# Prompt attention in 64 equal steps: query tiles m and 15-m of a head side by side, with the halves of q and k made in the projections

## What is computed

```python
def stick_breaking(q, k, v, sb_bias, q_pos, k_pos):
    z = jnp.einsum('bqhd,bkhd->bhqk', q.astype(jnp.float32), k.astype(jnp.float32)) * (HEAD_DIM_SB ** -0.5)
    z = z + sb_bias.astype(jnp.float32)[None, :, None, None]
    mask = k_pos[None, :] < q_pos[:, None]
    log_1mb = jnp.where(mask, jax.nn.log_sigmoid(-z), 0.0)
    suffix = lax.cumsum(log_1mb, axis=3, reverse=True) - log_1mb
    a = jnp.where(mask, jnp.exp(jax.nn.log_sigmoid(z) + suffix), 0.0)
    o = jnp.einsum('bhqk,bkhd->bqhd', a, v.astype(jnp.float32))
    return o.astype(v.dtype)
```

## Time and profile before

| | us |
|---|---|
| median of three runs | 3154.99 |
| the profiled execution | 3153.76 |
| its span | 3152.2 |
| attention, first logits to first matmul of the next stage | 547.78 to 1198.92 |
| PE busy over the span | 3035.5 (96%) |
| DVE, ACT busy over the span | 2062.2, 1645.0 |

### The profile page before, as it was taken

The page is one execution under the profiler, slowest core; times in us unless marked ns, Lnnn a source line. Parts: engine busy times, 40 slices in busy tenths (PEclk is TensorE's granted clock), DMA queues, the critical chain, the costliest instruction groups (busy, mean ns, idle before and its releaser), DMA issues.

```text
span 3152.2 us, 51506 instructions
## 1 busy us (share of the span) xinstructions
PE 3035.5 (96%) x18364; PEld 2805.3 (89%) x18364; DVE 2062.2 (65%) x2820; ACT 1645.0 (52%) x2375; POOL 149.1 (5%) x277
## 2 busy tenths in 40 slices
PE   8999999888888889999999999999999999999998
PEld 6888887776677669999999999999999999999998
DVE  4222422888987897775677756777477774778845
ACT  5444311997888885543445534455344543444433
POOL 0000000112311220000000000000000000000000
PEclk9999999999999999999999999999999999999999
DMA  5224334554755555443364334543445434444432
GB/s 185 93 93 137 108 114 120 139 135 133 202 129 134 137 169 156 118 120 112 110 183 120 114 114 130 164 119 111 116 142 154 115 113 117 143 127 120 115 112 78
DMA packets 584224, 405.90 MB, mean 129 GB/s; under 512 B 38489, under 2 KB 547842, under 8 KB 584034
## 3 DMA queue, kind: packets, MB, share of 16 engines
q1 hardware_dynamic: 543012, 301.45, 33.8%
q0 software_dynamic: 20544, 67.19, 7.4%
q10 hardware_dynamic: 20512, 35.17, 3.2%
HBM read 358.87 MB, written 44.87 MB: 128 GB/s over the span
## 4 chain that ended last, share of the span: by engine, by line
PE 62%; DVE 0%; issue 0%; DVEq 0%; ACT 0%; ACTq 0%
PE pf_acc L60 20%; PE pf_acc L58 20%; PE pf_acc L59 20%; PE pf_ps_t L1720 1%; PE pf_ps_sum L1659 0%; PE pf_ps_sum L1668 0%; PE pf_ps_sum L1673 0%; PE pf_ps_t L1730 0%; PE pf_ps_t L1791 0%; DVE late_c L2066 0%; DVE late_ssum L1998 0%; DVEq L1596 0%; DVE late_u L1988 0%; DVE pf_h L2192 0%; ACT late_sq L1819 0%
## 5 line engine op out<-in xcount | busy, mean ns | idle before, releaser
L1812 ACT ACTIVATE late_w_hi<-ahead_raw 128x1024 fp32r<-128x1024 f32 x439 | 463.8, 1057 | 536.7 <-PE pf_acc L60 533.9
L60 PE MATMUL pf_acc<-pf_x_hi,late_w_lo 128*128 128x416 f32 x2080 | 734.1, 353 | 0.0
L58 PE MATMUL pf_acc<-pf_x_hi,late_w_hi 128*128 128x416 f32 x2080 | 733.1, 352 | 0.0
L59 PE MATMUL pf_acc<-pf_x_lo,late_w_hi 128*128 128x416 f32 x2080 | 726.0, 349 | 0.0
L1982 DVE TENSOR_TENSOR late_w_lo<-ahead_raw,late_w_hi 128x1024 fp32r<-128x1024 f32 x439 | 536.1, 1221 | 269.8 <-ACT late_w_hi L1812 269.0
L58 PE MATMUL pf_acc<-late_f_hi,late_w_hi 128*128 128x416 f32 x1280 | 453.4, 354 | 3.2 <-DVEq L2205 3.2
L60 PE MATMUL pf_acc<-late_f_hi,late_w_lo 128*128 128x416 f32 x1280 | 451.9, 353 | 0.0
L59 PE MATMUL pf_acc<-late_f_lo,late_w_hi 128*128 128x416 f32 x1280 | 447.6, 350 | 0.0
L59 PEld LDWEIGHTS pf_acc<-pf_x_lo,late_w_hi 128*128 128x128 f32 x2080 | 390.8, 188 | 7.9 <-issue 1.6
L58 PEld LDWEIGHTS pf_acc<-pf_x_hi,late_w_hi 128*128 128x128 f32 x2080 | 390.5, 188 | 3.7 <-issue 1.6
L60 PEld LDWEIGHTS pf_acc<-pf_x_hi,late_w_lo 128*128 128x128 f32 x2080 | 390.0, 187 | 2.3
(11 more groups left out here) (248 smaller groups left out, 3971.9 us busy)
## 6 DMA issues: line engine op xcount, KB each, us to landing
ahead_raw<-in_w_up_dram SPq DMA_DIRECT2D x220, 512.0 KB, 4.0
ahead_raw<-in_w_down_dram SPq DMA_DIRECT2D x80, 512.0 KB, 4.0
high_pages<-in_cache_k_dram POOLq DMA_DIRECT2D x128, 256.0 KB, 3.5
ahead_raw<-in_w_out_dram SPq DMA_DIRECT2D x40, 512.0 KB, 5.3
ahead_raw<-in_w_ple_gate_dram SPq DMA_DIRECT2D x40, 512.0 KB, 4.0
high_pages<-in_cache_v_dram POOLq DMA_DIRECT2D x64, 256.0 KB, 3.4
at_kT<-in_cache_v_dram POOLq DMA_DIRECT2D x64, 256.0 KB, 4.1
ahead_raw<-in_w_down_dram SPq DMA_DIRECT2D x40, 384.0 KB, 3.5
```

The lines of the kernel that those rows point to most:

```text
L58: nc.tensor.matmul(out, stat_hi, mov_hi, start=first, stop=False)
L59: nc.tensor.matmul(out, stat_hi, mov_lo, start=False, stop=False)
L60: return nc.tensor.matmul(out, stat_lo, mov_hi, start=False, stop=last)
L1812: nc.scalar.activation(w_hi[k % 4][:, :], raw[k % 4][:, :], ACT.Copy).then_inc(hi_split, 1)
```

## The change

- A step has two query tiles of a head, m and 15-m, side by side in one row of 17 key blocks: the long tile's keys first, then the short one's. There are 64 steps of 2176 columns, in three pieces of 1024, 1024 and 128 (GRANULES). In heads 0 to 6 the pairs go from (7, 8) to (0, 15), in the last head the other way round.
- A logits chunk in which the border between the tiles lies is made in two parts. Each step has two running products and one multiplication. A result is copied out and stored after every two steps.
- The halves of q and k are made in the projection: `turned` casts and subtracts out of PSUM, four tensors QH, QL, KH, KL are stored, and `load_operands` loads them ready for use, 1536 keys of head 0 in the projection stage, the rest of it at the start of the attention, other heads whole. The raw buffers and all operand work in the attention are gone; so are the bias columns of each head.
- The sample units are spread evenly over steps 3 to 61. With two units in most iterations, eight sums fall into iterations 26 and 55 each.
- Turns and logits take turns (one group, one piece) instead of both pieces in a row, and the weighing of a pair comes right behind them.
- The work on the first tokens' mixture moves from iterations STEPS to STEPS+2 to iterations STEPS+LAG and behind, and its load waits for the stores of pairs 28 and 29.

```diff
 
+FIRST_KEYS = 1536
+
+
+def load_operands(eng, D, tiles, h, cols, loaded):
+
+    q2, k_hi, k_lo = (f32(t[:, cols]) for t in tiles)
+    rows = slice(64 * h, 64 * h + 64)
+    for part in range(2):
+        half = slice(64 * part, 64 * part + 64)
+        eng.dma_start(q2[half, :], D[("QH", "QL")[part]][rows, cols]).then_inc(loaded, 16)
+        eng.dma_start(k_hi[half, :], D["KH"][rows, cols]).then_inc(loaded, 16)
+        eng.dma_start(k_lo[half, :], D["KL"][rows, cols]).then_inc(loaded, 16)
+
+
...
-                sp.dma_start(dst[:, :, bass.ds(at, P)], src[s][:, :, :]).then_inc(stored[s], 16)
+                sp.dma_start(to_hi[:, :, bass.ds(at, P)], hi[s][:, :, :]).then_inc(stored[s], 16)
+                sp.dma_start(to_lo[:, :, bass.ds(at, P)], lo[s][:, :, :]).then_inc(stored[s], 16)
...
             def turned(n, s, which, stores):
-                signal, ready, src, dst, stored, own = (
-                    (k_turned, kT_ready, ps_kT, kT, kT_stored, keep["kT_s"]) if which == "k" else
-                    (q_turned, qT_ready, ps_qT, qT, qT_stored, keep["qT_s"]))
+                signal, high, ready, src, hi, lo, stored, own = (
+                    (k_turned, kT_high, kT_ready, ps_kT, kT, kT_lo, kT_stored, keep["kT_s"]) if which == "k" else
+                    (q_turned, qT_high, qT_ready, ps_qT, qT, qT_lo, qT_stored, keep["qT_s"]))
                 dve.wait_ge(signal, n + 1)
                 if isinstance(n, int) and n == 0:
                     nc.vector.tensor_copy(own[:, :, :], src[:, :].rearrange("p (k t) -> p k t", k=4)[:, :, 0:32]).then_inc(ready, 1)
                     return
                 if stores is not None:
-                    dve.wait_ge(stored[s], 16 * stores)
-                nc.vector.tensor_copy(dst[s][:, :, :].rearrange("p k t -> p (k t)"), src[:, :]).then_inc(ready, 1)
+                    dve.wait_ge(stored[s], 32 * stores)
+                banked = src[:, :].rearrange("p (k t) -> p k t", k=4)
+                nc.vector.tensor_copy(hi[s][:, :, :].bitcast(F32R), banked).then_inc(high, 1)
+                dve.wait_ge(high, n)
+                nc.vector.tensor_tensor(lo[s][:, :, :].bitcast(F32R), banked, hi[s][:, :, :], ALU.subtract).then_inc(ready, 1)
 
             prepare(0, 0, None, 16)
 
@@ -853,14 +869,7 @@
...
     HEADS, NQ, LAG = 8, 16, 3
-    STEPS = HEADS * NQ
+    PER = NQ // 2
+    STEPS = HEADS * PER
+    TILES, GRANULES, RUNS = NQ + 1, 3, 5
...
+    def short_tile(s):
+
+        return s % PER if s // PER == HEADS - 1 else PER - 1 - s % PER
+
+    def long_tile(s):
+        return NQ - 1 - short_tile(s)
...
-    total_keys = sum(keys_of(s) + 300 for s in range(3, STEPS - 2))
     units_of = [[] for _ in range(STEPS + LAG + 2)]
-    t, run, placed = 3, keys_of(3) + 300, 0
+    t, placed, first_unit, last_unit = 3, 0, 3, STEPS - 3
     for g in range(GROUPS):
         for u in range(UNITS):
             if apart(u) and units_of[t]:
-                for _ in range(2 if u in (U_TURN, U_MIX) else 1):
-                    t += 1
-                    run += keys_of(t) + 300
-            while t < STEPS - 3 and run * GROUPS * UNITS < placed * total_keys:
+                t += 2 if u in (U_TURN, U_MIX) else 1
+            while t < last_unit and (t + 1 - first_unit) * GROUPS * UNITS < placed * (last_unit - first_unit):
                 t += 1
-                run += keys_of(t) + 300
...
+    def turns(t):
 
         s = t - LAG
-        return min(groups[s], max(1, 3 - len(turned_fills(t)))) if has(s) else 0
+        if not has(s):
+            return [range(0)] * (GRANULES + 1)
+        first = max(1, 3 - len(turned_fills(t)))
+        ends = [first, first + 1, first + 2, RUNS]
+        return [range(a, b) for a, b in zip([0] + ends, ends)]
 
...
+                def load(h):
+                    if h >= 2:
+                        sp.wait_ge(z_ready, granule(PER * (h - 1), 0))
+                    load_operands(sp, D, [t[h % 2] for t in (q2, k_hi, k_lo)], h, slice(0, 2048), qk_loaded[h % 2])
 
                 def load_v(h):
                     sp.dma_start(v[h % 2][:, :, :].unsqueeze(2), v_src[:, :, h:h + 1, :]).then_inc(v_loaded[h % 2], 16)
...
+                def load_raw():
+                    sp.wait_ge(z_ready, granule(STEPS - PER, 0))
                     for n in range(4):
                         sp.dma_start(join["raw"][n][:, :].rearrange("p (k n) -> p k n", k=8),
                                      T["w_out"][0].rearrange("(k p) n -> p k n", p=P)[:, :, n * P:(n + 1) * P]).then_inc(join["raw_loaded"][n], 16)
-                    sp.wait_ge(half_ready, 2 * HEADS)
-                    sp.wait_ge(oT_stored[0], 32 * 2 * HEADS)
+
+                def load_mix():
+
+                    for n in range(2):
+                        sp.wait_ge(oT_stored[n], 32 + 32 * 15)
                     sp.dma_start(join["mix"][:, :, :], D["MIXT"].rearrange("(k p) t -> p k t", p=P)[:, :, 0:416]).then_inc(join["mix_loaded"], 16)
 
...
                     if h + 1 < HEADS:
-                        load(2 * h + 2)
+                        load(h + 1)
+                    else:
+                        load_raw()
...
-                        load(2 * h + 3)
-                    else:
-                        load_ahead()
-                    store(h, 2)
                     if h + 1 == HEADS:
                         wait_emptied(sp, ("mix", GROUPS - 1))
                         sp.dma_start(D["MIXT"][0:512, 2048:2080].rearrange("(k p) t -> p k t", p=P), mixT[:, :, :]).then_inc(mix_stored, 16)
+                        load_mix()
+                    store(h, 2)
...
                 def logits(s, g):
-                    i, h = s % NQ, s // NQ
-                    n = keys_of(s)
-                    if i == 0 and g == 0:
-                        pe.wait_ge(half_ready, 2 * h + 1)
-                    if i == 8 and g == 0:
-                        pe.wait_ge(half_ready, 2 * h + 2)
+                    h = s // PER
+                    if g == 0 and s % PER == 0:
+                        pe.wait_ge(qk_loaded[h % 2], 96 * (h // 2 + 1) + (96 if h and h % 2 == 0 else 0))
+                    if g == 0 and s == FIRST_KEYS // P - PER:
+                        pe.wait_ge(qk_loaded[0], 192)
                     at = granule(s, g)
                     z = ps_z[at % 2]
                     pe.wait_ge(b_done, at + 1)
-                    width = min(n - 1024 * g, 1024)
-                    for c in range(0, width, BANK):
-                        w = max(min(BANK, width - c), 2 * P)
-                        k0 = 1024 * g + c
-                        diagonal = k0 <= n - P < k0 + w
-                        q = q2[h % 2][:, i * P:(i + 1) * P]
-                        nc.tensor.matmul(z[:, c:c + w], q, k_hi[h % 2][:, k0:k0 + w], start=True, stop=False)
-                        last = nc.tensor.matmul(z[:, c:c + w], q, k_lo[h % 2][:, k0:k0 + w], start=False, stop=not diagonal)
-                        if diagonal:
-                            d = n - P - 1024 * g
-                            last = nc.tensor.matmul(z[:, d:d + P], ident_b[:, :], far_b[:, :], start=False, stop=True)
+                    border = P * (long_tile(s) + 1)
+                    for c in range(1024 * g, min(1024 * (g + 1), WIDTH), BANK):
+                        end = min(c + BANK, WIDTH)
+                        parts = [(c, min(end, border), long_tile(s), c)] if c < border else []
+                        if border < end:
+                            parts.append((max(c, border), end, short_tile(s), max(c, border) - border))
+                        parts.sort(key=lambda part: part[1] - part[0])
+                        for a, b, tile, k0 in parts:
+                            w, z0 = max(b - a, 2 * P), a - 1024 * g
+                            turned = b - a == P and b - c == BANK
+                            last = scores(z, z0 - P if turned else z0, w, q2[h % 2][:, tile * P:(tile + 1) * P], h, k0, turned, b in (border, WIDTH))
+                            if b in (border, WIDTH):
+                                last = nc.tensor.matmul(z[:, b - P - 1024 * g:b - 1024 * g], ident_b[:, :], far_b[:, :], start=False, stop=True)
                     last.then_inc(z_ready, 1)
 
                 def turn(s, r):
                     bank = claim(("turn", s, r))
-                    for kt in range(4 * r, min(4 * r + 4, s % NQ + 1)):
-                        last = nc.tensor.transpose(bank[:, kt % 4 * P:kt % 4 * P + P], rest[s % 4][:, kt * P:(kt + 1) * P], keep["ident"][:, :])
+                    for n in run_tiles(r):
+                        last = nc.tensor.transpose(bank[:, n % 4 * P:n % 4 * P + P], rest[s % 4][:, n * P:(n + 1) * P], keep["ident"][:, :])
                     last.then_inc(filled, 1)
 
...
-                    i, h, quad = s % NQ, s // NQ, s // 4
-                    if i == 0:
+                    h, pair = s // PER, s // 2
+                    if s % PER == 0:
```

(54 more changed lines are left out.)

211 lines of the change are left out of this document (74 added, 137 removed).

## The result

The changed kernel takes 3225.8 us (median of 4 runs, 3223.8 to 3227.8), the kernel before 3155.1: a ratio of 1.022 [1.021, 1.024], slower by 70.7 us. The forecast was 3145 us, and its range ended at 3180. The profiled run has a span of 3225.9 us (before 3152.2).

The account below looks back on a forecast made before the run. No single engine bounds the attention; the most loaded one changes twice in every head. Terms: -17.7 to the last logits, +5.4 attention end, +2 projection end, sum -10.3: 3145 us. Own range 3125 to 3160; with the large rivals 3105 to 3180.

Parts of the forecast that it names:

- One with eight sums on a heap (14): Attention, step into which the planner puts eight sums of the sample part: claimed to take 14 us.
- a heap that meets a weighing, 17: End of the attention, second heap of sums, in a step with a weighing: with two empty steps, put at 17 us.
- Heads' loads grow from 2 to 3 MB; they start four steps ahead, nothing.: Attention, operand loads on SP: start 40 us ahead, cost nothing; sharing engines with the pages 0 to 5 us, taken as 0.
- key step: Attention, 33 steps holding sample key units (1.94 a step): taken as 10.2 us each, ends 9.5 and 10.6, 337 us together.
- The layout: Two key steps laid out, with 0.2 us a hand-over and a weighing every second step: 21.2 us, 10.6 each.
- The step with the new rows: Attention, step for the sample part's new rows, occurring twice: 8 us each.
- that with the sample's scan: Attention, step with the sample scan, occurring twice: 11 us each, DVE 7.2 + 1.2 + 4.4, partly absorbed by its lead.
- End of the projection: Behind the projection's last matmul, two more operations of 0.7 us and one more issue: +2 us (1 to 3).
- End of the attention: Last logits to first token-stage matmul: mixture work moves behind ACT's last copies, 31.3 us against 25.9, +5.4 us (0 to 8).
- TensorE's additional 8 to 22 us: Attention, 46 pairs of logits matmuls a head instead of 40, more of them short: PE's need grows by 8 to 22 us.
- The lump decides: Rival, key steps: 10.6 us holds and PE's waits cost clock, 0.4 us more in 61 steps; 3180 us, chance 0.22.
- The levels even out: Rival, attention: every step runs like the old long half, ACT busy 94%, stage 568 us; 3105 us, chance 0.22.

Follow-up runs that it names:

- e2: Changed kernel without loading 96 of its 128 value pages; sums from the fifth of a group on reread the first four's pages; 3171.2 us, one run.
- e5: e1 with heads' operands from the third on loaded in three parts and the attention's first load on GpSimd's queue; 3169.8 us, ratio 1.004.
- e8: e1 with most of the weighing left out, only the first and last block of each tile multiplied (wrong result); 3140.5 us, one run.
- e9: e5 with two groups of weights turned, not one, ahead of the second logits in steps with sample key units; 3135.2 us, ratio 0.994.
- e6: Changed kernel (64 steps of pairs) without the sample part of the attention; 493.6 us first to last logits, 3030.8 us in all, one run.
- e4: Changed kernel with a pair's weighing cut in two, blocks 8 to 16 moved to the odd step between turn groups; 3227.6 us, ratio 1.023.
- e13: e9 with the weighing cut in two, the second half in the odd step ahead of the third group of turns; 3128.1 us, ratio 0.992.
- e12: Changed kernel with only the edit of e9, two groups of turned weights ahead of the second logits; 3199.5 us, ratio 1.014.
- e11: e3 with two groups of turned weights, not one, ahead of the first logits in steps with sample key units; 3161.5 us, ratio 1.002.
- e3: Kernel before with only the halves of q and k made in the projections, still 128 steps of single tiles; 3148.9 us, ratio 0.998.
- e7: e3 (128 steps of single tiles) without the sample part of the attention; 505.0 us first to last logits, 3038.3 us in all, one run.
- e1: Changed kernel with the sample part placed by a table, the sixteen sums two a step instead of heaps of eight; 3185.4 us, ratio 1.009.
- e10: e5 with two groups of turned weights, not one, in front of the first logits of a key step; 3140.5 us, ratio 0.995.

## Why the prediction was wrong

**The heap of eight sums: the step that failed.** "One with eight sums on a heap (14)", and "a heap that meets a weighing, 17". The heaps took 32.9 and 35.1 us. e2 measures 14.1 and 16.9 with the pages there, and a kernel 55 us faster. The sum was made of instructions of three engines only. That a sum needs four pages and that GpSimd issues them one by one stands in the kernel, but the prediction looked for pages only as a share of DMA bytes ("0 to 5 us, taken as 0"). That share was 0.56 in the heap: no bytes were short, the issue was. Before, at most three sums stood in one step and most stood alone, and TensorE waited 3.6 us for value pages in all, so the supply of 4.63 us a sum hardly showed. In the terms of the prediction, the time up to the last logits was 83 us too short (608 against 691.4): 37 in the two heaps, 25 in the eight steps with two sums behind them, 15 in the key steps, 10 in the steps below; the others gave 4 back.

**"Heads' loads grow from 2 to 3 MB; they start four steps ahead, nothing."** For the head itself nothing, for whoever shares the DMA engines up to 9.9 us in one wait. By e5 it is 15.6 us in nine steps and 11.1 in the stage, in the spread placement.

**The key step.** The layout gave 10.6 us, I took 10.2, the traces show 10.55 and 10.8: 15 us in 33 steps. I had discounted a calculation with the share of busy time in the old kernel (89%), which had another order of work. And the layout had only half of the cause. It asked which engine lacks work, and the weighing does bound its own steps (e8, 1.3 us there); it did not ask which bank is claimed next. The claim is three fills behind, and e9 shows 0.8 us a step in it. e9 comes below the forecast of 608 us up to the last logits, with 598.3, but by an order of turns that the forecast did not have.

**Smaller terms.** The step with the new rows took 11.3 us (8 in the sum), that with the sample's scan 12.8 (11): 10 us over both groups. End of the projection +4.7 against +2. End of the attention: 28.0 us, +2.1 against +5.4, mostly since the mixture landed 17.2 us after the last logits where I had 19 to 20; ScalarE waited 1.62 us for it:

```profile
1253.17 0.37 SPq L1086 DMA_DIRECT2D ahead_mix<-MIXT  x1
...
1261.13 0.55 ACT L1384 ACTIVATE late_c<-ahead_mix 128x416 f32<-128x416 f32 x1 [1.62 <-DMA ahead_mix<-MIXT]
```

**What was right.** The multiplications took 2.42 us (2.43). VectorE and ScalarE came within 8 us of the busy times forecast, though they fell less than said (by 47.4 and 8.7 us, not 58 and 17). VectorE left the bound, and empty steps run at VectorE's 7.1 us (7.2). The conversion in the projection stayed hidden. TensorE's additional 8 to 22 us did not come: in e9 its busy time is 544.1 us against 545.9. Of these, 16.8 us were at the clock's lower level, before 25.7 and in the changed kernel 77.0. If work there takes twice its time, an estimate, the busy time at the upper level alone would be 535.7, 533.0 and 534.0 us: the short matmuls cost 1 to 3 us, less than the least I had, and the 26.6 us more in the changed kernel were the clock's.

**The rivals.** "The lump decides" came nearest in size (3180), and its price of the clock came out (0.4 us a key step: one in four 1.7 longer), but by luck: it put the clock of a stretch with PE busy 87% between 0.89 and 1.00 and passed over a row of its own group, in which PE is busy 85% at 1.00. Its mechanism is there without the sample part (e6) and in the steps with a weighing (e8), but parting the lump gives nothing (e4) or 7 us (e13), so it is not what was lost. "The levels even out" is true by 11.4 us without the sample part. Pages behind 3 MB were in "a load comes late", with 0.06 and 3165 us at most; a supply that cannot follow a heap was in no rival.

**The account.** Of 70.7 us: supply of the pages 55 (e2, heaps and what stands behind them, a head's load among it), order of the turns 26 (e12), end of projection and of attention 7; against that the halves' 7 and pairing's own gain of 11. These are differences of runs, some of them single, and they overlap, so they need not sum. Open is why one key step in four lost clock, and e11.

## To carry to other kernels

When a planner gets half as many steps, work that was spread may pile up: check each pile against its supplier's pace (issues and ready buffers), not only against engines and bytes. Where engines hand over through few rotating banks, ask for every fill which copy frees its bank and what stands before that copy; moving one group by one place was worth 26 to 35 us, more than pairing (11) and the halves (7) by themselves. And if a step laid out by hand says 10.6, do not average it with the share of another order.

## What was not expected of the hardware

- GpSimd's page loads come one per 1.157 us in the heap (0.54 of the load itself and 0.62 ahead of it), with the DMA engines at a share of 0.56. Between two of them the kernel has GpSimd read the page's number from the table (`value_load`, L1126). In e5 it issues six loads with fixed addresses 0.5 us apart (506.91, 507.44 and on). So about half of the pace may be the reading; no run takes it away.
- An issue on SyncE's queue is held while megabytes stand before it: 2.03 us behind 1 MB and v, 5.0 to 5.5 behind 1.5 MB (e3, e7, e11), 8.6 to 10.1 behind 2.36 MB (the changed kernel, e1, e2, e4, e6, e8, e12). With the 2.36 MB in GpSimd's queue SyncE's issues were held too, up to 3.0 us (e5, e9, e10, e13).
- Eight matmuls of a sum took 1.94 us inside the heap, at 824.00 and 828.71, at a granted clock of 0.50 (824 to 826); at its start, at 814.87, sixteen took 1.92, at 1.00. Between the two TensorE had stood 4.81 us for a page. So its stall costs again in the work behind it. The Trainium skill, Perfetto Trace Analysis, section Matmul Optimizations, says that the engine scales its power with its use and that matmuls should therefore run back to back; the trace agrees, with sums that took twice as long.
